# Where the lower parts of the peer key and value blocks are computed: GpSimd or VectorE, in a two-block transformer kernel

## The reference, cut to what matters

```python
def peer(xn, w_q, sub_keys, u, v):
    q = (t @ w_q).reshape(n_tok, PEER_HEADS, 2, PEER_DKEY // 2)
    sc = jnp.einsum('thpd,hpnd->thpn', q, sub_keys)          # 8 heads x 2 x 128 scores a token
    s1, i1 = lax.top_k(sc[:, :, 0], 16)
    s2, i2 = lax.top_k(sc[:, :, 1], 16)
    cand = s1[..., :, None] + s2[..., None, :]               # 256 sums a head
    top_s, pos = lax.top_k(cand, 16)
    eidx = take_along_axis(i1 * 128 + i2, pos)               # one of 16384 experts
    gate = jax.nn.softmax(top_s, axis=-1)
    hid = jax.nn.gelu(einsum('td,thkd->thk', t, u[eidx]))
    return einsum('thk,thkd->td', gate * hid, v[eidx])
```

## Time and profile before

| | before |
|---|---|
| median of 3 runs (lowest to highest) | 3266.08 us (3265.84 to 3266.89) |
| profiled execution, first to last instruction | 3265.0 us |
| TensorE matmul busy | 3029.1 us (93%) |
| VectorE busy | 1948.2 us (60%) |
| ScalarE busy | 1286.5 us (39%) |
| GpSimd busy | 2136.7 us (65%), of it L496 2125.9 us in 863 instructions of 2466 ns |
| DMA | 474.73 MB, mean 145 GB/s |

### The profile page before, as it was taken

How to read it: one execution, slowest core, us unless ns; L and a number is a source line. 1 busy time by engine, 2 the same in 40 slices (tenths; PEclk the granted TensorE clock), 3 DMA queues, 4 the chain that set the end, 5 groups by cost and what they waited for, 6 DMA issues and landing times. The chain is left out here.

```text
span 3265.0 us, 61411 instructions
## 1 busy us (share of the span) xinstructions
PE 3029.1 (93%) x21410; PEld 2710.7 (83%) x21410; DVE 1948.2 (60%) x2864; ACT 1286.5 (39%) x1734; POOL 2136.7 (65%) x887
## 2 busy tenths in 40 slices
PE   8889999999999889999999998978889899999996
PEld 7689999988877789999997776758688689999994
DVE  2429667778867673956777887765663642222224
ACT  3335544433344434554443334434400133333332
POOL 6469866666677676986666667756201368888883
PEclk9899999999999999999999999989678899999998
DMA  5245544444445454554444444544100345555553
GB/s 199 90 155 174 174 144 145 142 136 148 144 163 169 148 171 152 174 173 140 143 141 136 145 144 161 167 163 155 52 14 27 129 136 180 174 179 174 175 178 103
DMA packets 129783, 474.73 MB, mean 145 GB/s; under 512 B 14576, under 2 KB 14720, under 8 KB 129440
## 3 DMA queue, kind: packets, MB, share of 16 engines
q1 hardware_dynamic: 126864, 461.95, 44.1%
q0 software_dynamic: 2544, 11.41, 0.9%
q10 hardware_dynamic: 288, 0.17, 0.0%
HBM read 472.42 MB, written 1.05 MB: 145 GB/s over the span
## 5 line engine op out<-in xcount | busy, mean ns | idle before, releaser
L496 POOL TENSOR_TENSOR wlo<-ring,whi 128x1024 fp32r<-128x1024 f32 x863 | 2125.9, 2466 | 1106.2 <-ACT whi L1085 869.7
L1085 ACT ACTIVATE whi<-ring 128x1024 fp32r<-128x1024 f32 x863 | 918.3, 1064 | 1762.1 <-PE prod L599 612.6
L598 PE MATMUL prod<-xh,whi 128*128 128x256 f32 x3960 | 1000.1, 289 | 25.0 <-ACT gains L1075 9.8
L599 PE MATMUL prod<-xl,whi 128*128 128x256 f32 x3960 | 985.9, 286 | 0.0
L598 PEld LDWEIGHTS prod<-xh,whi 128*128 128x128 f32 x3960 | 773.5, 195 | 31.3 <-DVEq L1385 10.1
L599 PEld LDWEIGHTS prod<-xl,whi 128*128 128x128 f32 x3960 | 771.8, 195 | 1.7 <-issue 0.5
L603 PE MATMUL prod<-xh,wlo 128*128 128x256 f32 x3960 | 560.7, 285 | 10.2 <-POOL wlo L496 10.2
L603 PEld LDWEIGHTS prod<-xh,wlo 128*128 128x128 f32 x3960 | 515.4, 194 | 12.1 <-POOL wlo L496 12.0
L1576 DVE TENSOR_TENSOR aux<-aux 128x256 bf16<-128x256 bf16 x256 | 410.6, 1604 | 44.4 <-ACT arena L1157 36.8
L1565 DVE TENSOR_TENSOR xl<-arena,xh 128x256 fp32r<-128x256 f32 x256 | 354.4, 1385 | 102.7 <-ACT xh L1183 102.7
L755 PE MATMUL acc<-whi,xh 128*128 128x512 f32 x1024 | 298.4, 413 | 39.1 <-DVE xl L1565 38.0
(11 more groups left out here) (289 smaller groups left out, 2702.5 us busy)
## 6 DMA issues: line engine op xcount, KB each, us to landing
ring<-in_peer_u SPq DMA_DIRECT2D x256, 512.0 KB, 3.5
ring<-in_peer_v SPq DMA_DIRECT2D x256, 512.0 KB, 3.5
ring<-in_exp_gate SPq DMA_DIRECT2D x64, 512.0 KB, 3.4
ring<-in_exp_up SPq DMA_DIRECT2D x64, 512.0 KB, 3.5
ring<-in_exp_down SPq DMA_DIRECT2D x64, 512.0 KB, 3.5
ring<-in_peer_q SPq DMA_DIRECT2D x32, 512.0 KB, 3.4
ring<-in_odd_in SPq DMA_DIRECT2D x24, 512.0 KB, 3.5
ring<-in_even_qk SPq DMA_DIRECT2D x16, 512.0 KB, 3.4
```

Of the source, the lines that this page charges most:

```text
L496: pool.tensor_tensor(wlo[:, s % PAIR, :], ring[:, g % RING, :], whi[:, s % PAIR, :].bitcast(F32), ALU.subtract)\
L598: pe.matmul(dst, w[:, k * P:(k + 1) * P], xh[:, k, :], start=(k == 0), stop=False)
L599: mm = pe.matmul(dst, w[:, k * P:(k + 1) * P], xl[:, k, :], start=False, stop=False)
L1085: act.activation(whi[:, s % PAIR, :], ring[:, g % RING, :], ACT.Copy).then_inc(hi_ready, 1)
```

## The change

GpSimd no longer makes the lower parts of key and value blocks. VectorE does, for all 256 blocks of each layer, with the same waits. In the first stretch its subtractions are dealt out between the routing operations by `Pace`: each routing operation adds its element count and 60 to an account, and each 1700 of it (SHARE) releases one subtraction, up to 51 (EARLY - 1). The others follow at fixed places: block 51 behind the scaled gates, 52 and 53 behind the copies of the turned results, up to 64 behind the first one-hots, and then one for each round of the loops. The indices are turned after key block 51 (EARLY = 52) instead of 55. ScalarE's Exp keeps its place (EARLY // RING - 1 is 12). In the second half with gates TensorE's token groups run one value block ahead, and on VectorE `chunk_rest` and the subtraction follow the gate multiplication of the round before.

```diff
...
+EARLY = 52
+SHARE = 1700
...
-            rests("peer_u0", 2 * NK)
...
-            rests("peer_u1", 2 * NK)
...
-                with pe.Fori(0, HALF // RING - 2) as i:
+                with pe.Fori(0, EARLY // RING) as i:
                     for j in range(RING):
                         hidden(i, j)
 
@@ -773,7 +773,7 @@
                     for n in range(3):
                         mm = pe.transpose(bank[:, n * P:(n + 1) * P], sel_i[:, n, x, :], ident)
                     mm.then_inc(gen_mm, 1)
-                for n in range(HALF - 2 * RING, HALF):
+                for n in range(EARLY, HALF):
                     hidden(0, n)
 
                 token_gates(0, 0, 0)
@@ -787,13 +787,18 @@
                     hidden(0, HALF + j)
 
                 acc_free()
+                token_gates(0, 0, 1)
                 for j in range(RING):
-                    token_gates(0, j, 1)
+                    token_gates(0, j + 1, 1)
                     down(0, j, first=(j == 0))
-                with pe.Fori(1, HALF // RING) as i:
+                with pe.Fori(1, HALF // RING - 1) as i:
                     for j in range(RING):
-                        token_gates(i, j, 1)
+                        token_gates(i, j + 1, 1)
                         down(i, j)
+                for j in range(HALF - RING, HALF):
+                    if j + 1 < HALF:
+                        token_gates(0, j + 1, 1)
+                    down(0, j)
                 with pe.Fori(HALF // RING, NK // RING - 1) as i:
                     for j in range(RING):
                         down(i, j)
...
-                early = 12
+                early = EARLY // RING - 1
...
-            def top16(vals, idx, src, n):
+            def top16(vals, idx, src, n, pace):
 
                 for r in range(2):
                     lo = slice(8 * r, 8 * r + 8)
                     for m in range(n):
                         c = dve.max(vals(m)[:, lo], src(m))
+                        pace.spent(src(m))
                     link(c)
                     for m in range(n):
                         c = dve.max_index(idx(m)[:, lo], vals(m)[:, lo], src(m))
+                        pace.spent(src(m))
                     if r == 0:
                         for m in range(n):
                             c = dve.match_replace(src(m), vals(m)[:, lo], src(m), -3.0e38)
+                            pace.spent(src(m))
                     link(c)
 
-            def route(x):
-                top16(lambda m: top_s[:, m, :], lambda m: top_u[:, m, :].bitcast(U32), lambda m: score[:, x, m, :], 16)
+            class Pace:
+
+
+                def __init__(self, rest):
+                    self.rest, self.done, self.owed = rest, 0, 0
+
+                def spent(self, ap):
+
+                    self.owed += int(np.prod(ap.shape[1:])) + 60
+                    if self.owed >= SHARE and self.done < EARLY - 1:
+                        self.owed -= SHARE
+                        self.upto(self.done + 1)
+
+                def upto(self, n):
+
+                    while self.done < n:
+                        self.rest(self.done)
+                        self.done += 1
+
+            def route(x, pace):
+                top16(lambda m: top_s[:, m, :], lambda m: top_u[:, m, :].bitcast(U32), lambda m: score[:, x, m, :], 16, pace)
                 dve.tensor_copy(top_f, top_u.bitcast(U32))
                 c4 = cand.rearrange("p h (a b) -> p h a b", b=TOPK)
                 link(dve.tensor_tensor(c4, wide(top_s[:, 0::2, :], 3, TOPK), wide(top_s[:, 1::2, :], 2, TOPK), ALU.add))
-                top16(lambda m: sel_s[:, x, m, :], lambda m: pos_u[:, m, :].bitcast(U32), lambda m: cand[:, m, :], PEER_H)
+                pace.spent(cand)
+                top16(lambda m: sel_s[:, x, m, :], lambda m: pos_u[:, m, :].bitcast(U32), lambda m: cand[:, m, :], PEER_H, pace)
                 for n, (op, by) in enumerate(((ALU.logical_shift_right, 4), (ALU.bitwise_and, TOPK - 1))):
                     link(dve.tensor_scalar(pos_a.bitcast(U32), pos_u.bitcast(U32), by, None, op))
                     link(dve.tensor_copy(pos_f, pos_a.bitcast(U32)))
                     flat = pos_f.rearrange("p h k -> p (h k)")
                     link(dve.tensor_tensor(pick, wide(iota[:, 0:TOPK], 1, P), wide(flat, 2, TOPK), ALU.is_equal))
+                    pace.spent(pick)
                     p4 = pick.rearrange("p (h k) a -> p h k a", k=TOPK)
                     link(dve.tensor_tensor(p4, p4, wide(top_f[:, n::2, :], 2, TOPK), ALU.mult))
+                    pace.spent(pick)
                     link(dve.tensor_reduce(sel_i[:, n, x, :], pick, AX, ALU.add))
+                    pace.spent(pick)
                 g = sel_i[:, 2, x, :].rearrange("p (h k) -> p h k", k=TOPK)
                 return dve.tensor_tensor(g, sel_s[:, x, :, :], wide(sel_s[:, x, :, 0], 2, TOPK), ALU.subtract)
 
             def peer(layer, last):
                 rms_norm(f"ffn{layer}", last)
                 take_split()
+                u, v = f"peer_u{layer}", f"peer_v{layer}"
+
+                def rest(name, b, i=0):
+
+                    g, s = BASE[name] + b, SPLIT[name] + b
+                    dve.wait_ge(hi_ready, s + 1 + RING * i)
+                    dve.wait_ge(w_used, SPLIT_BLOCKS[s - PAIR] + 1 + RING * i)
+                    dve.tensor_tensor(wlo[:, s % PAIR, :], ring[:, g % RING, :], whi[:, s % PAIR, :].bitcast(F32), ALU.subtract)\
+                        .then_inc(lo_ready[s % PAIR], 1)
+
+                pace = Pace(lambda b: rest(u, b))
                 for b in range(2):
                     for x in range(NX):
                         for q in range(2):
                             bank = group().rearrange("p (a b) -> p a b", b=NK)
                             link2(dve.tensor_copy(score[:, x, 8 * b + 4 * q:8 * b + 4 * q + 4, :], bank))
+                    pace.upto(b + 1)
                 for x in range(NX):
-                    last = route(x)
+                    last = route(x, pace)
                 last.then_inc(topk_ready, 1)
+                pace.upto(EARLY - 1)
 
                 dve.wait_ge(gate_exp, layer + 1)
                 gate = sel_i[:, 2, :, :].rearrange("p x (h k) -> p (x h) k", k=TOPK)
                 link(dve.tensor_reduce(st[:, 16:32], gate, AX, ALU.add))
                 link(dve.reciprocal(st[:, 32:48], st[:, 16:32]))
                 dve.tensor_tensor(gate, gate, wide(st[:, 32:48], 2, TOPK), ALU.mult).then_inc(normed, NX)
+                pace.upto(EARLY)
                 for x in range(NX):
                     bank = group()
                     tok = slice(x * P, (x + 1) * P)
                     dve.tensor_copy(hk[:, 0:2, tok], bank[:, 0:2 * P].rearrange("p (a b) -> p a b", b=P))
                     link2(dve.tensor_copy(gate_f[:, tok], bank[:, 2 * P:3 * P]))
+                    pace.upto(EARLY + x + 1)
 
                 for g in range(PARTS):
                     link(dve.tensor_copy(hk[:, 2 + g, :], gate_f))
@@ -1588,23 +1634,42 @@
                             .then_inc(gated, 1)
 
                     one_hots(0)
-                    dve.wait_ge(fm_out, FMBASE[f"peer_u{layer}"] + (half + 1) * HALF)
-                    with dve.Fori(0, HALF // RING - 1) as i:
-                        for j in range(RING):
-                            one_hots(j + 1, i)
-                            if half == 1:
-                                chunk_rest(j, i)
-                            gate_group(j, i)
-                    for j in range(HALF - RING, HALF):
-                        if j + 1 < HALF:
-                            one_hots(j + 1)
-                        if half == 1:
-                            chunk_rest(j, 0)
-                        gate_group(j)
+                    if half == 0:
+                        pace.upto(HALF + 1)
+                    dve.wait_ge(fm_out, FMBASE[u] + (half + 1) * HALF)
+                    if half == 0:
+                        with dve.Fori(0, HALF // RING - 1) as i:
+                            for j in range(RING):
+                                one_hots(j + 1, i)
+                                gate_group(j, i)
+                                rest(u, HALF + 1 + j, i)
+                        for j in range(HALF - RING, HALF):
+                            if j + 1 < HALF:
+                                one_hots(j + 1)
+                            gate_group(j)
+                            if j + 1 < HALF:
+                                rest(u, HALF + 1 + j)
+                        rest(v, 0)
+                    else:
+                        chunk_rest(0, 0)
+                        with dve.Fori(0, HALF // RING - 1) as i:
+                            for j in range(RING):
+                                one_hots(j + 1, i)
+                                gate_group(j, i)
+                                chunk_rest(j + 1, i)
+                                rest(v, j + 1, i)
+                        for j in range(HALF - RING, HALF):
```

(7 more changed lines are left out.)

## The result

The change is faster: a median of 3216.80 us (3213.41 to 3220.89, 4 runs) against 3266.16 (3265.84 to 3266.89, 4 runs) for the kernel before, measured beside it; a ratio of 0.9848 [0.9834, 0.9862]. That is 49.4 us less, where the prediction's sum had 22.8 less. The profiled execution took 3213.41 us, the fastest of the four, with a span of 3211.6 against 3265.0.

A forecast was written before the change was run, and what follows sets the result against it. TensorE paces the first stretch; GpSimd's subtraction blocks VectorE, so value blocks wait. From 3266.1 us, +37.6 - 3.0 - 4.0 - 4.6 - 48.8 = -22.8 gives 3243; 8 in 10 for 3224 to 3264.

The forecast's parts named there:

- What bounds, and why value blocks wait: TensorE paces the first stretch; in value blocks it waits 12.4 us for `xl`, held on VectorE by GpSimd's subtraction.
- First stretch, +18.8 a layer: Key blocks beside routing: VectorE becomes the bound, delaying the stretch by 18.8 us a layer, +37.6 in all.
- (a): First stretch: VectorE's routing without blocking would take 106.0 us a layer, with 30.8 of blocking gone.
- (b): First stretch: 49 subtractions fall inside routing on VectorE, with 2 before it.
- (c): Each subtraction on VectorE costs 1.17 us, bounds 1.15 and 1.30.
- (d): End of first stretch: TensorE's block 50 starts its last third 3.65 us after ScalarE is free for the gates' Exp.
- (e): Before block 50 TensorE idles some 6 us, then loses 1.2 us to the lower clock.
- Start of the halves, -3.0 and -4: Shorter one-hot stalls at the start of both gate halves: -1.5 a layer in the first, -2 in the second.
- Loop of the second half, 3.58 a step: Second half with gates: a chain through several engines gives 3.58 us a step, TensorE alone 3.46; -4.6 in all.
- Value blocks, 2.77: Value blocks alone: 2.77 us a block, bounds 2.73 and 2.85; -48.8 over both layers.
- The overlap of VectorE's operations: On VectorE, an operation starts some 0.08 us before the one in front ends, so a 1.23 us subtraction gives 1.15.
- Rival 1: All gains at their good ends, less clock cost: value blocks 2.73, second half near 3.5; 3223 us, chance 0.15.

The follow-up runs named there:

- experiment 1: Changed kernel with all subtractions back on GpSimd, keeping the new second-half order and the index turn at block 52: 3303.14 us.
- experiment 2: Changed kernel with the value blocks' subtractions back on GpSimd, key blocks' on VectorE: 3322.92 us.
- experiment 5: Changed kernel plus one GpSimd subtraction of dead data per value block, 60 a layer, its result read by nobody: 3337.81 us.
- Experiment 4: Changed kernel with only key blocks 0 to 63, those beside routing, back on GpSimd: 3195.88 us.
- Experiment 9: Experiment 4's kernel with VectorE's one-hots made one group further ahead in the second half: 3196.23 us.

## Why the prediction was wrong in size and right in direction

The step that failed is the price of the first stretch: +37.6 forecast, +22.6 measured. It is half of the error of 30.6 us between the two spans; the smaller half is that the second half with gates and the value blocks gained 68.9 instead of 57.4 (8.0 instead of 4.6 in the loop, 55.0 instead of 48.8 in the value blocks, 5.9 instead of 4 at the start).

- **What bounds, and why value blocks wait: right.** Experiments 1, 2 and 5 show it from three sides.
- **First stretch, +18.8 a layer: too dear by 7.5.** That VectorE's work sets the pace and the Exp's place passes it on was right; the place of TensorE's waits wasn't (14 waits for subtractions, the longest 2.5 us, in place of one of 6 us ahead of block 50), and five of the sizes weren't, all to the same side. (a) *Routing alone at 106.0*: the trace gives 395.91 - 237.23 - 48 x 1.15 = 103.5, 2.5 less, since more of its time had been blocking (33 us, not 30.8). (b) *49 subtractions*: 48, as an operation releases at most one even when it owes two, 1.2. (c) *1.17 for one*: 1.15, 1.0. (d) *Exp to block 50, 3.65 us after ScalarE is free*: the table load of 1.28 ran inside the wait, 1.35. (e) *6 us idle ahead of block 50, and 1.2 for the clock*: VectorE issues block 49's subtraction only at 394.49, so TensorE spends the time on block 49 and idles 1.21, and no block there is at the lower clock, 1.2. That is 7.25; layer 0 came out 7.1 below the forecast and layer 1 7.9, which wasn't taken apart. The bound "less than 12 us a layer" for being wrong is met (11.7 and 10.9).
- **That the loss is in the first stretch: right, and it could have been avoided.** Experiment 4 has the gain without it. The first stretch is bound by TensorE before, so freeing VectorE's neighbours there could bring nothing.
- **Start of the halves, -3.0 and -4: -5.6 and -5.9.** The direction was right. Down block 1 comes 6.8 us after token group 64 where it came 10.2 and 9.4 after. In the first half, the way from its first to its third token group went from 8.57 us (437.08 - 428.51) to 7.33 in layer 0, and from 9.84 (1490.31 - 1480.47) to 5.93 in layer 1; the other good end, the lower clock that may go too, came true in one layer.
- **Loop of the second half, 3.58 a step: 3.56 and 3.57, right for the wrong reason.** I had a chain through three engines at 3.58 and *"TensorE alone 3.46"*. Experiment 9 loosens that chain, and the step stays at 3.53: TensorE's own work is that long, 2.82 for the block and 0.71 for the token group. So the size was luck: the chain wasn't the bound, and the term that was, 3.46, was 0.07 short. With one step that no longer has a token group, the stage gave -8 instead of -4.6.
- **Value blocks, 2.77: 2.72.** Taken over 66 blocks from 900.52, (1079.94 - 900.52 - 0.71 + 0.91) / 66. *"I take 2.77"* was a middle between 2.73 and 2.83; the lower one was right, and the low row had shown it. 65 x 0.05 x 2 layers is 6.5 us.
- **The overlap of VectorE's operations, taken from rows: right.** The subtraction costs 1.15 from start to start for 1.22 of duration. The Trainium skill, "VectorE: DVE Perf Modes", section on the DRAIN you can't avoid, has the next operation start when the pipe is empty, but adds that one that isn't held starts earlier. The prediction set the page against the rows and left out that second sentence, with which this trace agrees.
- **Range.** Each term was given a middle value on the dear side, and the bounds of the first stretch stood in no range: I had bounds for the second half and the values alone. The errors added up (-15.0, -2.6, -11.5, -1.5 elsewhere) instead of cancelling. Rival 1 came nearest with 3223, but for half of the reason only: it kept the first stretch at +37.6.

## What to carry to other kernels

A GpSimd operation between parts of SBUF costs more than its own time: each kind of VectorE operation with two SBUF inputs that started under one here (`xl`, the one-hots, the subtraction) stood until it ended. Look for one VectorE line with two durations in two stretches, and move the GpSimd work where the waiting line is on the chain, and only there. Before such a move, ask stretch by stretch which engine is the bound: beside routing VectorE was nearly full and the same move was a loss. And when terms are worked out one by one with a choice in each, check that the choices don't all lean to one side.

## What the runs showed of the hardware

- An operation on GpSimd that shares no data with VectorE still lengthens it, up to 3.41 us for one of 1.21 (experiment 5), longer than either alone.
- Not every VectorE operation is held. In the kernel before, L1587, which reads one input from SBUF and one from PSUM, started 248 times inside an L496 and took 0.42 us at the median, as without it. But the CAST L1525, whose one input is in SBUF, took 2.38 us, each time inside an L496, and takes 0.23 now (L1553).
- ScalarE's table load of 1.28 us for the next function ran while the function's own instruction was still waiting for its input: here it cost nothing, as ScalarE was early.
- A block with a token group ahead of it takes 0.10 us more than one without, though nothing waits. By what, stays open.
- After a stall of 1.28 and 1.35 us in the two layers, the way from the first to the third token group took 7.33 us in one, with part of it at the lower clock, and 5.93 in the other, at the full one; in experiment 4 it is the other way round, 5.86 in layer 0 and 7.43 in layer 1. What decides stays open.
- The runs of all versions with VectorE's subtractions scatter by 2 to 8 us, those of the kernel before by 1 to 4.4. That wasn't followed up either.
